# First key tile of the prompt at 128 columns instead of 64 in both softmax attentions, its padding masked through a bias row, and two masks dropped

## What is computed

```python
def _fox_attend(q, k, v, c_q, c_k, pos_q, pos_k):        # forgetting attention, 4 heads of 64
    s = jnp.einsum('bqhd,bkhd->bhqk', q, k) * (HD_B ** -0.5)
    s = s + (c_q[..., :, None] - c_k[..., None, :])      # cumulative log forget, per key and head
    s = jnp.where((pos_k[None, :] <= pos_q[:, None])[None, None], s, -jnp.inf)
    p = jax.nn.softmax(s, axis=-1).astype(v.dtype)
    return jnp.einsum('bhqk,bkhd->bqhd', p, v)

def _dsa_attend(q, k, v, iq, ik, iw, cid_q, cid_k, k_top):   # sparse, one shared key/value head
    sc = jnp.einsum('bqhd,bkd->bqhk', iq, ik)
    score = jnp.einsum('bqhk,bqh->bqk', jax.nn.relu(sc), iw) * IDX_SCALE
    score = jnp.where((cid_k[None, :] <= cid_q[:, None])[None], score, -jnp.inf)
    _, sel = lax.top_k(score, min(k_top, k.shape[1]))        # k_top = 256
    # softmax attention of the query over the selected, admissible keys only
```

## Time and profile before

| | |
|---|---|
| median of 3 runs | 2413.31 us (2410.1 to 2415.28) |
| the profiled execution | 2407.27 us |
| its span, first to last instruction | 2405.3 us |
| TensorE matmul busy | 2186.8 us, 91% of the span |
| VectorE busy | 1484.6 us, 62% |
| ScalarE busy | 643.1 us, 27% |
| GpSimd busy | 328.1 us, 14% |
| attention of the first layer | about 557 to 845 us of the span |
| attention of the second layer | about 1749 to 2036 us |

### The profile page before, as it was taken

The page is one execution under the profiler, slowest core; times in us unless marked ns, Lnnn a source line. Parts: engine busy times, 40 slices in busy tenths (PEclk is TensorE's granted clock), DMA queues, the critical chain, the costliest instruction groups (busy, mean ns, idle before and its releaser), DMA issues. The chain is left out here.

```text
span 2405.3 us, 27372 instructions
## 1 busy us (share of the span) xinstructions
PE 2186.8 (91%) x9906; PEld 1331.1 (55%) x9930; DVE 1484.6 (62%) x3125; ACT 643.1 (27%) x1478; POOL 328.1 (14%) x418
## 2 busy tenths in 40 slices
PE   4999999997999968889959999999989999789887
PEld 3544444466777755545445444444667677545554
DVE  3357999995545454654333589999955454564651
ACT  3333001113333323232143420010133333233331
POOL 0000000000000043543200000000000001353541
PEclk9999999998999968998979999999989999698988
DMA  7111322213022020221051113222120220111211
GB/s 276 63 65 62 114 73 72 66 39 69 12 81 76 1 96 22 90 87 62 36 174 49 64 67 110 72 76 66 42 62 7 82 75 31 66 64 49 97 53 55
DMA packets 144006, 169.95 MB, mean 71 GB/s; under 512 B 68560, under 2 KB 106192, under 8 KB 143600
## 3 DMA queue, kind: packets, MB, share of 16 engines
q1 hardware_dynamic: 118400, 135.52, 17.6%
q10 hardware_dynamic: 25472, 32.66, 3.8%
HBM read 115.53 MB, written 62.50 MB: 74 GB/s over the span
## 5 line engine op out<-in xcount | busy, mean ns | idle before, releaser
L767 PE MATMUL ps<-wring,xnT_arena 128*128 128x512 f32 (+3 forms) x2304 | 883.0, 540 | 0.0
L767 PEld LDWEIGHTS ps<-wring,xnT_arena 128*128 128x128 f32 x2304 | 430.7, 190 | 431.4 <-issue 369.4
L1483 DVE TENSOR_SCALAR_CACHE_REDUCE arena<-arena,theta 32x1056 bf16<-32x1056 f32 x496 | 471.6, 987 | 8.8
L1065 PE MATMUL ps<-arena 128*128 128x128 f32 (+1 forms) x632 | 134.4, 343 | 100.2 <-DVE arena L1671 84.3
L1571 DVE TENSOR_REDUCE small<-ps 128x1 f32<-128x192 f32 (+9 forms) x148 | 114.1, 771 | 154.9 <-PE ps L942 148.3
L1065 PEld LDWEIGHTS ps<-arena 128*128 128x128 f32 x632 | 103.1, 213 | 188.6 <-DVE arena L1671 142.8
L1009 PE MATMUL ps<-wring,arena 128*128 128x512 f32 x320 | 172.8, 662 | 5.7 <-DVE arena L1612 5.7
L1176 ACT COPY arena<-ps 128x512 f32<-128x512 f32 (+2 forms) x96 | 51.2, 533 | 464.4 <-PE ps L767 464.4
L1468 DVE SCALAR_TENSOR_TENSOR arena<-arena,iw 128x512 f32<-128x512 f32 (+6 forms) x224 | 135.7, 606 | 57.3 <-ACT arena L1231 50.4
L1324 ACT ACTIVATE arena<-ps,small 128x192 f32<-128x192 f32 (+9 forms) x148 | 111.0, 750 | 159.5 <-DVE small L1571 159.4
L1009 PE MATMUL ps<-wring,xnT_arena 128*128 128x512 f32 x256 | 135.1, 652 | 0.0
(11 more groups left out here) (239 smaller groups left out, 2670.7 us busy)
## 6 DMA issues: line engine op xcount, KB each, us to landing
wring<-in_w_in SPq DMA_DIRECT2D x24, 1024.0 KB, 7.7
projected<-arena ACTq DMA_DIRECT2D x96, 256.0 KB, 2.0
arena<-residual SPq DMA_DIRECT2D x36, 512.0 KB, 5.6
arena<-projected SPq DMA_DIRECT2D x36, 384.0 KB, 3.8
arena<-projected SPq DMA_DIRECT2D x18, 512.0 KB, 5.9
residual<-arena SPq DMA_DIRECT2D x18, 512.0 KB, 2.7
wring<-in_w_out SPq DMA_DIRECT2D x8, 1024.0 KB, 6.5
out<-arena SPq DMA_DIRECT2D x16, 512.0 KB, 3.9
```

The source lines that it names most:

```text
L767: o = mm(bank(pbank(k), 0, wide), xnT[:, c, t * P:(t + 1) * P], w, start=(c == 0), stop=(c == CH - 1))
L1065: o = mm(bank(level_bank(k), 2 * n_ * g, 2 * n_), keys[:, g * P:(g + 1) * P], queries[:, :, g, :], start=True, stop=True)
L1483: V.tensor_scalar(cmp_out[r, (i % 2) * WMAX:(i % 2) * WMAX + uw[u]], score[u][r], th_, 0.0, op, ALU.add, accum_out=into[r, i:i + 1]).then_ ...
```

## The change

The first key piece becomes a whole tile of 128 columns, at PSUM column 384, so that the keys are 1152 columns wide instead of 1088 (`key_width`). Of tile 0 only rows 48 to 63 are real keys; the others are now shut out by the bias row. For the forgetting attention GpSimd writes -BIG into `negc` for those rows before the key tiles get their bias column; for the sparse attention it writes -BIG into row 64 of `dsaKT`. `nometa` goes, and its 64 columns leave the packed constants. `dsaown` goes for tiles 2 to 8, where `pen` already shuts those keys out; tile 2 has 320 keys of which for the first half of the queries fewer than 256 are admissible, so `pen` gets a memset there. The selection's own widths (`width`) stay at 64 + 128 t, so `pen` is read at a shifted place.

```diff
+def key_width(t):
+    return P + P * t
...
-        relu = [cut([WMAX]) for _ in range(2)]
+        WK = key_width(NT - 1)
+        relu = [cut([WK]) for _ in range(2)]
...
-        foxKT = ca([H, WMAX])
+        foxKT = ca([H, WK])
...
-        dsaKT = {"p": cn([WMAX]), "s": cn([SW])}
+        dsaKT = {"p": cn([WK]), "s": cn([SW])}
...
-            return [(0, HALF, 512 - HALF)] + [(HALF + P * j, P, 512 + P * j) for j in range(u)]
+            return [(P * j, P, 512 + P * (j - 1)) for j in range(u + 1)]
...
                                 if key == 0:
-                                    own = {"fox": "foxmeta", "dsa": "dsameta"}[m] if u == 0 else "nometa"
-                                    adds.append((CB("identb"), CB(own), 0, HALF))
-                                if u > 0 and key + w == width(u):
+                                    own = {"fox": "foxmeta", "dsa": "dsameta"}[m]
+                                    if u == 0:
+                                        adds.append((CB("identb"), CB(own), 0, HALF))
+                                if u > 0 and key + w == key_width(u) and (m == "fox" or u == 1):
                                     adds.append((CB("identb"), CB("causal" if m == "fox" else "dsaown"), w - P, P))
                                 if m == "dsa" and u >= 2:
-                                    adds.append((CB("identb"), pen[u][:, key:key + w], 0, w))
+                                    scored = (0, HALF) if key == 0 else (key - HALF, key - HALF + w)
+                                    adds.append((CB("identb"), pen[u][:, scored[0]:scored[1]], 0, scored[1] - scored[0]))
...
-                    if j == 0:
-                        copy(dsaKT["p"][0:HD, 0:HALF], ps[0:HD, 512 * b:512 * b + HALF]).then_inc(own_sem, one_more(own))
-                        return copy(dsaKT["p"][0:HD, HALF:HALF + 3 * P], ps[0:HD, 512 * b + P:512 * b + 4 * P])
                     n_ = min(NT - j, 4) * P
-                    return copy(dsaKT["p"][0:HD, width(j - 1):width(j - 1) + n_], ps[0:HD, 512 * b:512 * b + n_])
+                    return copy(dsaKT["p"][0:HD, P * j:P * j + n_], ps[0:HD, 512 * b:512 * b + n_])
...
                         o = V.tensor_scalar(pen[u][r], keep, 0.0, -BIG, ALU.is_equal, ALU.mult)
+                        if u == 2:
+
+                            o.then_inc(dve_own, one_more(own))
+                            dve.wait_ge(dve_own, own[0])
+                            o = V.memset(pen[u][0:HALF, w - HALF:w], -BIG)
                         o.then_inc(pen_done, 1)
...
+                    nc.gpsimd.memset(dsaKT["p"][HALF:HALF + 1, 0:SMETA], -BIG).then_inc(pool_own, one_more(own))
+                    nc.gpsimd.memset(dsaKT["p"][HALF:HALF + 1, HALF:P], -BIG).then_inc(pool_own, one_more(own))
+                    pool.wait_ge(pool_own, own[0])
...
                     pool.wait_ge(lf_negc, 1)
+                    nc.gpsimd.memset(negc[0:SMETA, NCACHE + 1], -BIG).then_inc(pool_own, one_more(own))
+                    nc.gpsimd.memset(negc[HALF:, NCACHE + 1], -BIG).then_inc(pool_own, one_more(own))
+                    pool.wait_ge(pool_own, own[0])
```

More of the change, by code:

```diff
@@ L114, in constants @@
     b["dsaown"] = -BIG * ((r[:, None] < 64) & (r[None, :] >= 64))
-    b["nometa"] = np.repeat(-BIG * (np.arange(HALF) < SMETA)[None, :], P, 0)
     c0 = np.arange(HALF)
@@ L257, in encoder @@
         pbuf = relu
-        cn_at = sum(uw.values()) + 2 * WMAX
+        cn_at = sum(uw.values()) + 2 * WK
         stage_at = cn_at + NT * NIX + WMAX + NS + SW + 2 * NI * P + 4 * D
@@ L1106, in copy_keys @@
                         rows = NS if u == "s" and j == NCACHE else P
-                        col = (P * j if u == "s" else max(0, width(u - 1))) if u != 0 else 0
-                        n_ = HALF if u == 0 else rows
+                        col = P * j if u == "s" else P * u
+                        n_ = rows
                         return copy(foxKT[0:HD + 1, :, col:col + n_], ps[0:HD + 1, 512 * b:512 * b + 512].rearrange("p (h n) -> p h n", h=H)[:, :, 0:n_])
```

## The result

| | before | after |
|---|---|---|
| median | 2412.91 us (2410.1 to 2415.28, 4 runs) | 2375.06 us (2372.26 to 2379.31, 4 runs) |
| span of the profiled execution | 2405.3 us | 2370.7 us |
| first to last start of the attention, layer 1 | 557.66 to 844.11 = 286.45 us | 558.02 to 827.54 = 269.52 us |

The ratio is 0.9851 [0.9832, 0.987], 38 us less by the medians. I had forecast 2409.0 us, 4.3 less, with a range down to 2401: the direction was right, the size was wrong by a factor of nearly nine, and the time lies outside the range.

The account below looks back on a forecast made before the run. PE was taken to bound the attention, except where tiles 0 and 4 wait on a ring of engines. PE -5.9, ring +1.1 and entry +0.5 gave -4.3 us: 2409.0 us from the median 2413.31, range 2401 to 2420.

Parts of the forecast that it names:

- Turns and value product: First key tile in attention: wider stationary operands, 128 instead of 64, in the same number of instructions, costed at nothing.
- the free widening: Rival, chance 0.22: widening the first score pair costs nothing, the 7.2 us drop out, -11.5 us in all, 2401.8 us.
- The chain takes over: Rival, chance 0.07: tiles 1 and 5 also come to wait for DVE, losing PE's gain there; -2.2 us, 2411.1 us.
- The prices on PE: Attention's score pairs and masks, priced by start-to-start spacing on PE; in sum -5.9 us.
- All loads are hidden: Rival, chance 0.11: masks never delay weight loads in attention scores, and wider pairs cost all their streaming; +10.4 us, 2423.7.
- The masks: Attention scores: dropped pad and chunk masks save their own spacing, and some following pairs come 0.09 us sooner; -13.1 us.
- Widening: First score pair of every attention job, 64 to 128 columns: +0.05 us a job, 144 jobs, +7.2 us.
- The ring of tiles 0 and 4: Engines in turn pace these coupled attention tiles; wider maximum and exp cost 0.07 on each of 16 couples, +1.1 us.
- The entry: Start of attention, waiting for DVE's key buffer fill: longer fill, a memset and a wait, +0.26 a layer, +0.5 us.

Follow-up runs that it names:

- the three comparisons of runs: Masks dropped from the kernel before (0.9971); the same with value product at 128 rows (0.9827), against that product alone (0.9884); masks put back into the kernel after (0.9917).
- the 92 us: Span of the kernel after, 2370.7 us, against 2278.6 with the recurrences' 128-row products written first and the 64-row ones behind; that version measured 2282.39 us, 0.9469.
- the regrouped ones: Kernel after with each recurrence tile's eight 128-row products first, then its eight 64-row ones, start flag only on each PSUM bank's first product: 2282.39 us, 0.9469.

## Why the prediction was wrong

**The step that failed** is *Turns and value product*: "So I cost the wider ones at nothing", and for the product "its 64-row pair stands in the same stream of 0.1125 a matmul". What I had read was a slope. The two rows give 0.85 us for 6 and 1.75 for 14; the slope between them is 0.1125, but 6 x 0.1125 = 0.675 and 14 x 0.1125 = 1.575. Both products were 0.175 us longer than their own matmuls at that price. This remainder was the border, and it stood on two rows that I quoted; the single starts above show it, 0.09 and twice 0.05 inside the product, and 0.09 more ahead of it. The rows after have none to speak of: 0.67 and 1.51 give 0.105 a matmul and 0.04 over. So the step failed in a term that it put at nothing: measured, 0.27 to 0.33 us in the jobs shown, 33.6 us over all 144, 37 us of time. For the turn, nothing was right.

A second view of the kernel before says the same, and I had passed over it: the groups of weight loads by shape (busy, mean ns | idle of the load path ahead of them, and its cause).

```profile
L979 PEld LDWEIGHTS ps<-arena,xnT_arena 128*128 128x128 f32 x576 | 70.7, 195 | 4.4
...
L979 PEld LDWEIGHTS ps<-arena,xnT_arena 64*128 64x128 f32 x144 | 21.4, 186 | 15.8 <-issue 15.8
```

The 144 loads of 64 rows, two a job, had 15.8 us of idle time ahead of them with nothing to wait for, 0.11 us each; the 576 loads of 128 rows had 4.4 us, 0.008 each. The idle time marks the way in; its size is not the matmul's 0.09, since in the trace loads run beside matmuls. The Trainium skill, "TensorEngine Tiling (Array Packing)", section "Key Properties", says that changing the tiling mode drains TensorE, and its section "Available Configurations" counts 64 rows as a mode of its own. The traces agree for rows, by 0.27 to 0.33 us for a 64-row pair between 128-row ones and by none at 96 rows; a turn of 64 columns, which that page also lists as a mode, cost nothing here. Read beside the 64-row pair, that sentence would have made this the first rival.

Nothing in my rivals held the border and the range ended with the free widening, at 2401. That rival leaned on the same rows of the value product and took their slope for a price that its 64-row pair shared.

**What the engines beside it took back.** The two stretches show 22.6 and 275.89 - 253.90 = 22.0 us less PE busy time, masks and widening included, and 5.6 and 5.0 us more idle. The waits of PE in the kernel after, 570 to 828 us (who, for whom: total, times, longest):

```profile
PE ps L960 <- ACT arena L1327: 4.8, 11, 0.7
PE ps L946 <- DVE xnT_arena L1128: 4.5, 10, 0.6
```

The stall of the earlier trace rows, 2.6 us in 6, has become 4.5 in 10, and the turns now wait 4.8 us for exponentials on ACT. PE gave a quarter of its gain back to the engines beside it. Six of the ten stalls are those of tiles 0 and 4, now 3.5 us. The other four are new and stand in tiles 1 and 5, two in each attention, such as this one:

```profile
605.31 1.54 PE L946 MATMUL ps<-xnT_arena,arena 128*128 128x128 f32 x6 [0.26 <-DVE xnT_arena L1128]
```

So the rival *The chain takes over* had the right couple and the right mechanism. It came in beside the gain, not in its place, and it had a PE gain of some 1 us to take back where the border gave more.

**What held.**
- The prices on PE. My signs were a first score pair of 0.22 us until a pair behind it and a 384 pair of 0.64. The trace shows 639.27 to 639.50, 0.22, and from there to the mask at 640.14 0.65, where it was 0.17 and 0.73 before. Where the scores follow a value product the first pair takes 0.276 (640.87 to 641.15), which I had called the sign of hidden loads; but there the 64-wide pair had taken 0.224 (645.85 to 646.08, the last row here, of the kernel before). It is 0.05 more in both places, as forecast, so in these jobs neither *The widening is free* nor *All loads are hidden* is borne out.

```profile
639.50 0.49 PE L946 MATMUL ps<-xnT_arena,arena 128*128 128x384 f32 x1
...
641.15 0.59 PE L946 MATMUL ps<-xnT_arena,arena 128*128 128x512 f32 x1
...
646.08 0.19 PE L942 MATMUL ps<-cb 128*128 128x64 bf16 x1
```

- The masks: forecast -13.1; the three comparisons of runs give 7 (8 either way), 14 (20) and 16 us (8). The starts agree with a weight load that a mask of 0.03 us cannot hide: the 384 pair is 0.08 us shorter without the mask ahead of it. The count held too, 72 masks of 128 columns:

```profile
L948 PE MATMUL ps<-cb 128*128 128x128 bf16 x72 | 15.8, 219 | 0.0
```

- Widening, ring and entry together: forecast 7.2 + 1.1 + 0.5 = 8.8, measured about 6, with 7 either way. *All loads are hidden* wanted 15.4 + 1.6 = 17.
- The ring of tiles 0 and 4: the stall before the next scores was to grow from 0.40 by 0.1. It grew by 0.2. In this ring none of the border's gain arrived: two couples take 9.59 us before (581.48 to 591.07) and 9.66 after (580.13 to 589.79). The first row is of the kernel before, the others of the kernel after:

```profile
581.48 0.41 PE L940 MATMUL ps<-xnT_arena,arena 128*128 128x64 f32 x2 [0.50 <-DVE xnT_arena L1125]
...
580.13 1.32 PE L946 MATMUL ps<-xnT_arena,arena 128*128 128x128 f32 x4 [0.56 <-DVE xnT_arena L1128]
...
585.04 1.32 PE L946 MATMUL ps<-xnT_arena,arena 128*128 128x128 f32 x4 [0.60 <-DVE xnT_arena L1128]
...
589.79 1.32 PE L946 MATMUL ps<-xnT_arena,arena 128*128 128x128 f32 x4 [0.60 <-DVE xnT_arena L1128]
```

- The entry: the fill was to last 1.98 us, and did; ahead of it stand 0.54 instead of 0.51 us. The attention starts 0.36 us later than before, against 0.26 forecast.

```profile
555.26 1.98 DVE L1544 MEMSET xnT_arena<- 64x2304 f32 x1 [0.54 <-DVE arena L1533]
557.28 1.06 ACT L1115 COPY xnT_arena<-ps 65x512 f32<-65x512 f32 x2 [8.26 <-DVE xnT_arena L1544]
```

Without the border, then, nothing speaks against the forecast of -4.3 us: the kernel after with its value product narrow is at 1.0004 [0.9968, 1.0039], and -4.3 us is 0.9982.

## What to carry to other kernels

Fit a line through two rows of different length and read both of its numbers: the slope is the price of one more instruction, the intercept is what the sequence pays to begin, end or change kind, and an edit that "only" changes a shape acts on the intercept. Look for matmuls of up to 64 rows between full ones, by the distance from their start to the next and by the idle time ahead of their weight loads in the groups by shape; pad them with zeros to the full height, or write them behind one another so that the border is crossed once. When PE sets the pace, a large gain there is partly given back to the engines just behind it, here a quarter.

## What the runs showed of the hardware

- A pair with a stationary operand of 64 rows between pairs of 128 costs TensorE 0.27 to 0.33 us over its own stream in the jobs shown: 0.09 at each crossing and 0.05 inside the pair behind it. Over all 144 jobs it came to 0.23 a job, since some wait for other engines anyway. With 96 rows it costs nothing that shows (0.9854 against 0.9851), with 32 rows the distances are those of 64, and 64 columns at 128 rows cost nothing that shows.
- 64-row pairs behind one another are cheap: sixteen matmuls in 880.32 - 879.24 = 1.08 us, 0.135 a pair, where the 128-row pairs ahead of them take 1.93 / 8 = 0.24. That was part of the 92 us and I had not expected it. The heads come in the order 0, 2, 1, 3, two in the lower half of the rows and two in the upper; whether the halves have to do with it was not tried.
- Alternating pairs cost 0.36 us each at the upper level of the clock and 0.62 at the lower, and behind the regrouped ones the lower level did not come in the tile shown. The division of the 92 us into border and clock above is an estimate; no run holds the clock still.
